# Taking 48 instead of 32 of 256 tokens out of the dense expert products, with GpSimd and ScalarE on the new 16, and first-key one-hots stored and reloaded

## The chip, the core and the metric

One Trainium2 chip, one core. The metric is the device time of the one launch in microseconds; lower is better.

## The reference

The network has three stages on 256 tokens of width 2048: an HGRN2 layer with a forgetting-attention layer, a second mixing layer (a gated linear recurrence and attention on selected keys), and a layer of product-key experts (PEER). The change is in the last one. Per token, 8 heads each choose 16 of 128 x 128 = 16384 experts by two keys of 128; each chosen expert is one row of `u` and one of `v`:

```python
expert = jnp.take_along_axis(cand_i, pos, axis=-1).reshape(t, -1)      # 128 of 16384 per token
gate = jax.nn.softmax(top_s, axis=-1).reshape(t, -1)
z = jnp.einsum('cd,ced->ce', xc, u[ec])
act = jax.nn.gelu(z, approximate=False) * gc
return jnp.einsum('ce,ced->cd', act, v[ec])
```

## The kernel before

**Dense tokens.** The kernel doesn't gather rows for most tokens. For the first DENSE = 224 tokens it computes z with *all* 16384 experts on TensorE, multiplies by a gate that is zero except at the chosen experts, and multiplies the result with all of `v`. The experts lie in four blocks of 32 units (BJ = 32; a unit is 128 experts x 2048 values, 1 MB fp32). The order is U0, U1, V0, U2, V1, U3, V2, V3; a U block makes z, the V block of the same number adds the output.

**A unit's way.** SP loads it into one of four buffers `raw` (`load`, L488), as soon as TensorE has finished the unit four before. ScalarE copies it to a rounded high half `wh` (L1344), VectorE subtracts to get the low half `wl` (L1856), and TensorE multiplies in single-pass fp32r: `dots` (L1142) has, per 128 rows, one matmul with `wh` and the high and low halves of x side by side (2 x 224 = 448 columns, L1153) and one with `wl` (224 columns, L1154). V0, V1 and V3 do the same (`wide_products`, L1201: L1206, L1207); V2 (`paired_v_block`, L1283) uses three matmuls of 224 columns (`value_products`, L1196 to L1198), two sums to a bank. Everything here has its own in-order queue per engine and meets by semaphores.

**Gates.** The gate of all experts of a block for 8 tokens is an outer product: `spread` (L1110) multiplies `hot_a` (one-hot of the first key, 128 slots x 8 tokens x 128 keys, fp16) with `gates_b` (one-hot of the second key within the block, times the gate) on TensorE, 8 matmuls of 64 columns, one turn ahead of each unit's products. With TURNS = 28 turns the 224 dense tokens of a block are done in 28 of 32 units. Gates of block b are spread during U(b+1), those of block 3 during V2. VectorE builds `hot_a`, `hot_b` and `gates_b` two turns ahead (`hot_rows`, L2534, `gate_rows`, L2547) and multiplies the spread gates onto the activations (`gate`, L2554), with ScalarE's copy of their low part (`keep_low_gates`, L1761). `hot_a` doesn't depend on the block, and is made anew in each.

**The last 32 tokens** (LAST) go by rows. Four groups of 32 partitions hold them, each group 32 of a token's 128 experts (ROWS = 32). `fetch_row` (L624) has GpSimd gather half rows (128 x 4 KB, into one of two buffers), and VectorE's `take_row` (L2607) takes a dot product with x (for u) or adds the weighted row to a sum (for v): 128 such steps, at turns listed by hand in ROW_TURNS (L60). `row_sums` (L1134) adds the four groups by a matmul with `token_of`, `add_rows` (L2641) puts them into x; the lower half of the width during V2, the upper at V3's end.

In V blocks ScalarE's loop (`v_highs`, L1815) also copies the activations' high half a unit ahead (`act_high`), and VectorE's `v_turns` (L2690) has their low half. In U blocks GpSimd adds the two halves of z (`add_dots`, L618), ScalarE applies GELU (`gelus`, L1774).

## Time and profile before

| | us |
|---|---|
| median of 3 runs | 3151.75 |
| runs | 3145.31, 3151.75, 6184.49 |
| profiled execution: time | 3146.41 |
| profiled execution: span | 3144.4 |

The span runs from the first to the last instruction. Times in rows are from its start. In the trace, PE is TensorE's matmul stream, PEld its weight loads, DVE is VectorE, ACT is ScalarE, POOL is GpSimd, SPq and POOLq are queues that issue DMAs. A timeline row is one instruction (or several of one kind, merged, xN): start, length, engine, line, operation, output <- inputs, shapes, and in brackets the engine's idle time before it with what ended it. Lengths of matmuls include their overlap with the next, so the distance of two starts is the time that one costs.

The table by stretch has one row per stretch: from:to, its length, then busy time and number of instructions of PE, PEld, DVE, ACT and POOL, the granted TensorE clock as a share of full speed, the mean busy share of the 16 DMA engines, and GB/s. A group row ends with busy us, mean ns of one, and idle time before.

### The profile page before, as it was taken

How to read it: one execution, taken by the hardware profiler on the slowest of the kernel's cores; microseconds unless marked ns; L12 is line 12 of the kernel's file. 1: busy time of each engine (PE TensorE's matmuls, PEld its weight loads, DVE VectorE, ACT ScalarE, POOL GpSimd, SP SyncE). 2: the span in 40 equal slices, each digit the busy share in tenths (PEclk: the TensorE clock that was granted, in tenths of full speed). 3: DMA queues.
4: the chain of work that ended last, by engine and by line, in shares of the span. 5: the costliest groups of instructions: out<-in, count | busy, mean ns of one | idle time of the engine just before them, and what ended most of it. 6: DMA issues, size and time to landing. Idle time of an engine off the chain costs nothing.

```text
span 3144.4 us, 62060 instructions
## 1 busy us (share of the span) xinstructions
PE 3106.8 (99%) x24748; PEld 3003.6 (96%) x24748; DVE 2407.6 (77%) x3908; ACT 1743.9 (55%) x2400; POOL 308.2 (10%) x303
## 2 busy tenths in 40 slices
PE   9999999999999999999999999999999999999998
PEld 9999999999999999999999988999999999999997
DVE  8767777755556776666668999988799789988887
ACT  6444545777776655555655455554555545554454
POOL 2000000000000000000000022331133112210110
PEclk9999999999999999999999999999999999999999
DMA  5444435444444545555455555678867787665785
GB/s 203 147 160 148 169 115 211 161 169 163 160 164 171 185 168 182 176 180 177 164 188 180 185 199 202 245 264 287 297 236 251 274 287 249 244 214 188 259 291 194
DMA packets 117821, 637.37 MB, mean 203 GB/s; under 512 B 11633, under 2 KB 32497, under 8 KB 50417
## 3 DMA queue, kind: packets, MB, share of 16 engines
q1 hardware_dynamic: 98496, 565.49, 50.7%
q0 software_dynamic: 18864, 68.43, 6.7%
q8 instruction: 121, 1.98, 0.2%
q10 hardware_dynamic: 288, 1.05, 0.1%
q14 instruction: 52, 0.42, 0.0%
HBM read 632.57 MB, written 2.36 MB: 202 GB/s over the span
## 4 chain that ended last, share of the span: by engine, by line
PE 86%; DVE 8%; DVEq 2%; ACT 2%; DMA 1%; issue 1%; ACTq 0%; SPq 0%
PE bank L670 14%; PE bank L672 14%; PE bank L671 14%; PE bank L1153 11%; PE bank L1206 9%; PE bank L1154 5%; PE bank L1207 5%; DVE wl L1856 3%; PE bank L1196 2%; PE bank L1198 2%; PE bank L1197 2%; PE bank L1117 1%; PE bank L824 1%; PE bank L1156 1%; ACT wh L1344 1%
## 5 line engine op out<-in xcount | busy, mean ns | idle before, releaser
L1856 DVE TENSOR_TENSOR wl<-raw,wh 128x1024 fp32r<-128x1024 f32 x1052 | 1267.1, 1238 | 349.9 <-ACT wh L1344 341.1
L1344 ACT ACTIVATE wh<-raw 128x1024 fp32r<-128x1024 f32 x1052 | 1052.7, 1050 | 394.3 <-DMA raw<-w_in_a 128.6
L671 PE MATMUL bank<-hhl,wh 128*128 128x256 f32 x3568 | 989.1, 277 | 0.0
L670 PE MATMUL bank<-hhl,wh 128*128 128x256 f32 x3440 | 966.9, 281 | 1.0 <-DVE hhl L1904 1.0
L672 PE MATMUL bank<-hhl,wl 128*128 128x256 f32 x3440 | 953.4, 277 | 0.0
L671 PEld LDWEIGHTS bank<-hhl,wh 128*128 128x128 f32 x3568 | 673.4, 189 | 1.9 <-issue 1.7
L670 PEld LDWEIGHTS bank<-hhl,wh 128*128 128x128 f32 x3440 | 647.9, 188 | 5.1 <-issue 2.4
L672 PEld LDWEIGHTS bank<-hhl,wl 128*128 128x128 f32 x3440 | 647.2, 188 | 0.0
L1153 PE MATMUL bank<-hhl,wh 128*128 128x448 f32 x1920 | 625.0, 382 | 6.8 <-DVE wl L1856 6.7
L1154 PE MATMUL bank<-hhl,wl 128*128 128x224 f32 x2048 | 522.4, 265 | 0.0
L1206 PE MATMUL bank<-ahl,wh 128*128 128x448 f32 x1488 | 472.1, 374 | 2.4 <-DVE ahl L2570 2.1
L1153 PEld LDWEIGHTS bank<-hhl,wh 128*128 128x128 f32 x1920 | 361.5, 188 | 40.6 <-DVE wl L1856 7.3
L1207 PE MATMUL bank<-ahl,wl 128*128 128x224 f32 x1536 | 400.1, 266 | 0.0
L1154 PEld LDWEIGHTS bank<-hhl,wl 128*128 128x128 f32 x2048 | 392.0, 191 | 2.8
L1206 PEld LDWEIGHTS bank<-ahl,wh 128*128 128x128 f32 x1488 | 279.5, 188 | 26.6 <-DVE ahl L2570 4.1
L1207 PEld LDWEIGHTS bank<-ahl,wl 128*128 128x128 f32 x1536 | 293.1, 191 | 1.5
L622 POOL TENSOR_TENSOR act<-z_parts 128x224 f32<-128x224 f32 x64 | 61.9, 967 | 1966.2 <-ACT z_parts L1785 1966.1
L1785 ACT ACTIVATE z_parts<-bank 128x448 f32<-128x448 f32 x128 | 69.8, 545 | 274.5 <-PE bank L1156 272.2
L670 PE MATMUL bank<-kh,wh 128*128 128x256 f32 x528 | 150.7, 285 | 0.0
L672 PE MATMUL bank<-kh,wl 128*128 128x256 f32 x528 | 147.0, 278 | 0.0
L671 PE MATMUL bank<-kl,wh 128*128 128x256 f32 x528 | 147.0, 278 | 0.0
L1196 PE MATMUL bank<-ahl,wh 128*128 128x224 f32 x512 | 142.8, 279 | 0.0
(461 smaller groups left out, 4405.2 us busy)
## 6 DMA issues: line engine op xcount, KB each, us to landing
raw<-peer_u SPq DMA_DIRECT2D x128, 1024.0 KB
raw<-peer_v SPq DMA_DIRECT2D x128, 1024.0 KB
raw<-w_in_c SPq DMA_DIRECT2D x64, 1024.0 KB
raw<-w_in_a SPq DMA_DIRECT2D x63, 1024.0 KB
raw<-w_kv SPq DMA_DIRECT2D x32, 1024.0 KB
raw<-w_in_b SPq DMA_DIRECT2D x32, 1024.0 KB
raw<-w_out_a SPq DMA_DIRECT2D x16, 1024.0 KB
raw<-w_out_b SPq DMA_DIRECT2D x16, 1024.0 KB
```

Source lines behind the costliest of these rows:

```text
L670: eng.matmul(out, h_[:, k, :], high[:, k, :], start=(k == 0), stop=False)
L671: eng.matmul(out, h_[:, k, :], low[:, k, :], start=False, stop=False)
L672: last = eng.matmul(out, low_rows(c, k), high[:, k, :], start=False, stop=(k == KC - 1))
L1153: eng.matmul(wide, wh[c % RAW][:, k, :], hhl[:, :, k, 0:DENSE], start=(k == 0), stop=False)
L1154: last = eng.matmul(wide[:, 0:DENSE], low_rows(c, k), hd[:, k, :], start=False, stop=False)
L1196: eng.matmul(out_, w_h, a_h, start=opens and e == 0, stop=False)
L1197: eng.matmul(out_, w_h, a_l, start=False, stop=False)
L1206: eng.matmul(wide, w_h, both, start=first, stop=False)
L1207: last = eng.matmul(wide[:, 0:DENSE], w_l, a_h, start=False, stop=False)
L1344: eng.activation(high_half(c, half), raw_half(c, half), ACT.Copy).then_inc(hi_ready, 1)
L1785: eng.activation(z_parts[:, c % 2, :], B[DOT_BANK[b] + c % 2][:, 0:2 * DENSE], ACT.Copy).then_inc(s["z_step"], 1)
L1856: eng.tensor_tensor(low_half_out(c, half), raw_half(c, half), high_half(c, half).bitcast(F32), ALU.subtract).then_inc(lo_ready, 1)
```

## The change

- MORE = 16 further tokens leave the dense products: DENSE is 208, TURNS 26. Matmuls of 448 columns have 416, those of 224 have 208.
- The 16 tokens go by rows, in 8 groups of 16 partitions (16 experts each, MORE_ROWS = 16), 64 gathers of 128 half rows into a single buffer `rows_more`. For u, GpSimd multiplies the 1024 columns with `x_more` (`more_dot`) and ScalarE sums the product with a copy's accumulator; for v, ScalarE scales the row and GpSimd adds it (`more_sum`). The steps stand at turns of the V blocks given by MORE_TURNS: 20 in V0, 21 in V1, 13 in V2, 10 in V3. ScalarE's part (`weigh_more`) comes at the end of its turn and waits for GpSimd's.
- SP copies keys and gates of these tokens in 16 small DMAs ahead of U1, and their x in 8 ahead of V0. Small tables move into the unused columns of `ahl`.
- `hot_a` is built in block 0's turns only. SP stores each tile (256 KB) to DRAM during U1, and reloads it in U2, U3 and V2 (`store_hot`, `load_hot`). A reload for turn n - 2 is issued behind the load of unit n; `spread` waits for it.
- The row sums of the new tokens are 8 more matmuls in each `row_sums`.
- Some semaphores of an earlier stage are merged into counting ones.

```diff
-DENSE = T - LAST
+MORE = 16
+MORE_GROUPS = P // MORE
+ROWED = LAST + MORE
+DENSE = T - ROWED
 TURNS = DENSE // TG
 ROWS = SLOTS_PER_TOKEN // GROUPS
+MORE_ROWS = SLOTS_PER_TOKEN // MORE_GROUPS
+ALL_ROWS = ROWS + MORE_ROWS
 ROW_TURNS = {
...
+MORE_TURNS = {
+    "V0": [n for n in range(BJ) if n % 8 in (0, 2, 3, 5, 6)],
+    "V1": [n for n in range(16) if n % 4 != 3] + [n for n in range(20, 30) if n != 24],
+    "V2": [n for n in range(13) if n % 2 == 0] + [n for n in range(20, BJ) if n % 2 == 0],
+    "V3": [n for n in range(23) if n % 5 in (0, 2)],
+}
...
+            def store_hot(n):
+
+                eng.wait_ge(sQ["pairs_ready"], n + 1)
+                eng.sem_inc(sp_passed, 1)
+                eng.dma_start(hot_rows_of[n], hot_tile(n)).then_inc(hot_stored[n % 2], 16)
+
+            def load_hot(b, n):
+
+                if (b, n) == (1, 0):
+                    for k in range(2):
+                        eng.wait_ge(hot_stored[k], 16 * (TURNS // 2))
+                eng.wait_ge(sQ["g_done"], b * TURNS + n - 1)
+                eng.sem_inc(sp_passed, 1)
+                eng.dma_start(hot_tile(n), hot_rows_of[n]).then_inc(hot_in[n % 2], 16)
+
+            def block_with_hot(name, table, b):
+
+                last = BLOCKS - 1 if name == "V" else b - 1
+                for n in range(BJ):
+                    load(n // PER_PAIR, BASE[f"{name}{b}"] + n % PER_PAIR, one(table, b * BJ + n))
+                    if 2 <= n < TURNS + 2 and last == 0:
+                        store_hot(n - 2)
+                    elif 4 <= n < TURNS + 2:
+                        load_hot(last, n - 2)
+                    elif TURNS + 2 <= n < TURNS + 4 and last < BLOCKS - 1:
+                        load_hot(last + 1, n - 2 - TURNS)
+
...
+                if (name, b) == ("U", 1):
+                    eng.wait_ge(sQ["x_out"], 16)
+                    eng.wait_ge(sQ["slots_step"], 1)
+                    eng.sem_inc(sp_passed, 1)
+                    for q in range(MORE_GROUPS):
+                        slots = slice(q * MORE_ROWS, (q + 1) * MORE_ROWS)
+                        eng.dma_start(row_keys[q * MORE:(q + 1) * MORE, :, ROWS:ALL_ROWS],
+                                      place[P - ROWED:P - LAST, NT - 1, :, slots]).then_inc(sQ["keys_in"], 16)
+                        eng.dma_start(row_gate[q * MORE:(q + 1) * MORE, ROWS:ALL_ROWS],
+                                      tops[P - ROWED:P - LAST, NT - 1].rearrange("p h k -> p (h k)")[:, slots]).then_inc(sQ["keys_in"], 16)
...
+            def fetch_more(g):
+
+                kind, r = g // MORE_ROWS, g % MORE_ROWS
+                eng.indirect_dma_start(out=rows_more[:, :], out_offset=None, in_=peer_u_rows if kind < 2 else v_rows,
+                                       in_offset=bass.IndirectOffsetOnAxis(ap=left[kind // 2][:, kind % 2, ROWS + r:ROWS + r + 1], axis=0)).then_inc(more_in, 16)
+
+            def more_dot(g):
+
+                kind, r = g // MORE_ROWS, g % MORE_ROWS
+                eng.wait_ge(more_in, 16 * (g + 1))
+                if g > 0:
+                    eng.wait_ge(sQ["more_by_scalar"], g)
+                if r == 0 and kind == 0:
+                    eng.wait_ge(sQ["more_x_in"], 16 * MORE_GROUPS)
+                if r == 0 and kind == 1:
+                    eng.wait_ge(sQ["x_out"], 16 + 16 * MORE_GROUPS)
+                eng.tensor_tensor(more_scaled[:, :], rows_more[:, :], x_more[:, :], ALU.mult)
+                eng.drain().then_inc(sQ["more_by_gpsimd"], 1)
...
+                fetch_more(g + 1)
...
+            def more_sum(g):
+
+                r = g % MORE_ROWS
+                in_place, ends = g in MORE_IN_PLACE, r == MORE_ROWS - 1
+                eng.wait_ge(sQ["more_by_scalar"], g + 1)
+                if not in_place and not ends:
+                    fetch_more(g + 1)
+                if r > 0:
+                    eng.tensor_tensor((rows_more if ends else x_more)[:, :], (rows_more if in_place else more_scaled)[:, :], x_more[:, :], ALU.add)
+                eng.drain().then_inc(sQ["more_step" if ends else "more_by_gpsimd"], 1)
+                if in_place and not ends:
+                    fetch_more(g + 1)
...
+                if b > 0:
+                    eng.wait_ge(hot_in[c % 2], i * (16 * PER_PAIR // 2) + 16 * (((b - 1) * TURNS + c) // 2 + 1))
...
+                eng.wait_ge(s["more_step"], f + 4)
+                for c in range(FH):
+                    eng.matmul(B[bank][:, FH * LAST + c * MORE:FH * LAST + (c + 1) * MORE], rows_more[:, c * P:(c + 1) * P],
+                               token_more[:, :], start=True, stop=True)
...
+            def weigh_more(b, n):
+
+                if (f"V{b}", n) in MORE_AT:
+                    g = MORE_AT[f"V{b}", n]
+                    kind, r = g // MORE_ROWS, g % MORE_ROWS
+                    if kind < 2:
+                        eng.wait_ge(s["more_by_gpsimd"], g + 1)
+                        eng.activation(more_scaled[:, :], more_scaled[:, :], ACT.Copy,
+                                       accum_out=row_dot[:, kind, ROWS + r:ROWS + r + 1]).then_inc(s["more_by_scalar"], 1)
+                    else:
+                        eng.wait_ge(more_in, 16 * (g + 1))
+                        if kind == 2 and r == 0:
+                            eng.wait_ge(s["more_step"], 3)
+                        elif r > 1 and g not in MORE_IN_PLACE:
+                            eng.wait_ge(s["more_by_gpsimd"], g - (kind - 2))
+                        out_ = x_more if r == 0 else rows_more if g in MORE_IN_PLACE else more_scaled
+                        eng.activation(out_[:, :], rows_more[:, :], ACT.Copy, scale=row_act[:, ROWS + r:ROWS + r + 1]).then_inc(s["more_by_scalar"], 1)
...
-                eng.tensor_tensor(hot_a[c % 2][:, :, :, :], iota_h[:, :, :].unsqueeze(1).broadcast_to(ka),
-                                  token_pairs[:, 0].unsqueeze(2).broadcast_to(ka), ALU.is_equal)
+                if b == 0:
+                    if n > 1:
+                        eng.wait_ge(hot_stored[c % 2], 16 * (n // 2))
+                    eng.tensor_tensor(hot_a[c % 2][:, :, :, :], iota_h[:, :, :].unsqueeze(1).broadcast_to(ka),
+                                      token_pairs[:, 0].unsqueeze(2).broadcast_to(ka), ALU.is_equal)
```

## Rows read from the trace of the kernel before

**Rows 1.** The page, busy time by engine, and the chain that ended last.

```profile
PE 3106.8 (99%) x24748; PEld 3003.6 (96%) x24748; DVE 2407.6 (77%) x3908; ACT 1743.9 (55%) x2400; POOL 308.2 (10%) x303
...
PE 86%; DVE 8%; DVEq 2%; ACT 2%; DMA 1%; issue 1%; ACTq 0%; SPq 0%
```

**Rows 2.** Stretches: busy us (instructions) by engine, granted clock, DMA share; U0 to V3.

```profile
1764.40:1940.90 176.50, 169.69 (x1065) 157.14 (x1063) 163.49 (x394) 93.50 (x141) 32.13 (x36) 0.99 0.56 195
1940.90:2113.00 172.10, 172.06 (x1250) 159.97 (x1249) 159.31 (x251) 97.03 (x158) 62.25 (x50) 1.00 0.70 248
2113.00:2275.00 162.00, 161.70 (x1024) 153.25 (x1024) 130.21 (x172) 81.62 (x97) 29.80 (x30) 1.00 0.84 292
2275.00:2447.00 172.00, 172.00 (x1249) 159.97 (x1248) 162.99 (x248) 95.85 (x155) 58.97 (x49) 1.00 0.71 250
2447.00:2609.30 162.30, 162.17 (x1025) 153.26 (x1024) 128.74 (x150) 81.57 (x98) 23.65 (x23) 1.00 0.79 279
2609.30:2781.30 172.00, 172.00 (x1252) 160.06 (x1252) 161.31 (x228) 96.23 (x155) 50.45 (x46) 1.00 0.69 246
2781.30:2963.60 182.30, 182.30 (x1777) 181.72 (x1777) 158.58 (x244) 87.69 (x126) 8.49 (x8) 1.00 0.58 204
2963.70:3129.00 165.30, 163.30 (x1042) 154.93 (x1040) 134.65 (x155) 86.70 (x111) 24.76 (x23) 1.00 0.74 259
```

**Rows 3.** Timeline of PE in V0: start us, length, ...; 448 and 224 columns in turn.

```profile
2149.90 0.37 PE L1206 MATMUL bank<-ahl,wh 128*128 128x448 f32 x1
...
2152.40 0.37 PE L1206 MATMUL bank<-ahl,wh 128*128 128x448 f32 x1
```

**Rows 4.** Timeline of PE in V2, 24 matmuls of 224 columns.

```profile
2899.75 0.27 PE L1196 MATMUL bank<-ahl,wh 128*128 128x224 f32 x1
...
2902.32 0.27 PE L1198 MATMUL bank<-ahl,wl 128*128 128x224 f32 x1
```

**Rows 5.** Timeline of PE: two of 512 columns and what follows; 13 of 256.

```profile
632.37 0.39 PE L879 MATMUL bank<-sum_h,ones_r 128*128 128x512 f32 x1
...
632.84 0.20 PE L657 MATMUL bank<-ones 128*128 128x64 f16 x1
...
1000.05 0.28 PE L670 MATMUL bank<-hhl,wh 128*128 128x256 f32 x1
...
1001.47 0.28 PE L670 MATMUL bank<-hhl,wh 128*128 128x256 f32 x1
```

**Rows 6.** Timelines of SP, ACT and PE: weight loads, issued and used.

```profile
1097.15 0.33 SPq L494 DMA_DIRECT2D raw<-w_iquery  x1
...
1101.94 2.01 ACT L1344 ACTIVATE wh<-raw 128x1024 fp32r<-128x1024 f32 x2 [2.44 <-DMA raw<-w_iquery]
...
2334.56 0.24 PE L1117 MATMUL bank<-gates_b,hot_a 128*128 128x64 f16 x2
...
2334.96 0.33 SPq L494 DMA_DIRECT2D raw<-peer_u  x1
...
2341.41 1.06 ACT L1344 ACTIVATE wh<-raw 128x1024 fp32r<-128x1024 f32 x1 [0.69 <-DMA raw<-peer_u]
```

**Rows 7.** Timelines of POOL and DVE: GpSimd's adds, and subtractions with and without them.

```profile
12.71 1.29 POOL L603 TENSOR_TENSOR sq<-first_sq 128x512 f32<-128x512 f32 x1 [3.67 <-ACT first_sq L1353]
...
19.27 5.75 POOL L603 TENSOR_TENSOR sq<-sq,first_sq 128x512 f32<-128x512 f32 x3 [5.28 <-ACT first_sq L1353]
...
23.79 3.44 DVE L1856 TENSOR_TENSOR wl<-raw,wh 128x1024 fp32r<-128x1024 f32 x2
...
2206.91 2.36 DVE L1856 TENSOR_TENSOR wl<-raw,wh 128x1024 fp32r<-128x1024 f32 x2
```

**Rows 8.** Timelines of POOL and DVE: one gather, issued and used.

```profile
2439.77 1.69 POOL L631 DMA_INDIRECT rows<-peer_u_rows,row_of  x1 [1.54 <-DVE rows L2618]
...
2443.36 1.23 DVE L2618 SCALAR_TENSOR_TENSOR rows<-rows,x_half 128x1024 f32<-128x1024 f32 x1 [1.58 <-DMA rows<-peer_u_rows,row_of]
```

**Rows 9.** Groups of DVE instructions in U2: the first-key compares.

```profile
L2544 DVE TENSOR_TENSOR hot_a<-iota_h,slotT 128x1024 f16<-128x1024 f16 x28 | 19.0, 680 | 0.0
```

More of the change, by code:

```diff
@@ L72 @@
         ROW_AT[_k, _n] = len(ROW_AT)
+assert len(ROW_AT) == 4 * ROWS
+MORE_TURNS = {
[4 more added lines that the diff above has]
+}
+MORE_AT = {}
+for _k, _v in MORE_TURNS.items():
+    for _n in _v:
+        MORE_AT[_k, _n] = len(MORE_AT)
+assert len(MORE_AT) == 4 * MORE_ROWS
+MORE_GELU_AT = 17
+MORE_GATED_AT = 17
+MORE_IN_PLACE = range(MORE_AT["V2", 0], MORE_AT["V3", 0])
 X_ROWS_AT = 9
```

189 lines of the change are left out of this document (126 added, 63 removed).

## The prediction

> **What bounds the kernel now.** I read the page first: TensorE is busy for 99% of the span and holds 86% of the chain that ended last, VectorE 8% of it [rows 1]. A TensorE that is always busy need not bound every stage, so the next view is the table by block of the expert stage [rows 2], cut where TensorE changes from one block of tables to the next (in order U0, U1, V0, U2, V1, U3, V2, V3). The reader is to see three kinds of stage. In U0 TensorE is busy 169.7 of 176.5 us and VectorE 163.5: VectorE's routing is the chain there. In U1, U2 and U3 TensorE is full and VectorE is nearly full too (159.3 to 163.0 of 172). In V0, V1, V2 and V3 TensorE is full, VectorE has 20% spare and the DMA queues are busiest (0.84 in V0). The granted clock is 1.00 in all (the 2.4 GHz level; 0.99 in U0). The 1,764 us before U0 aren't touched but for renamed semaphores, which I cost at nothing: each step waits for the same producer.
>
> **TensorE's columns.** In U0 to U3, V0, V1 and V3 the work is pairs of one 448-column and one 224-column matmul. From the first row of [rows 3] to the last lie eight pairs in 2.50 us: 313 ns a pair. They become 416 and 208 columns. What a wide column costs: two matmuls of 512 columns take 0.47 us together [rows 5], 235 ns each; of the 313 ns, if the narrow one has about 104, the wide one has 209. So 64 columns cost 26 ns, and 32 fewer save 13 ns. What a narrow column costs: 12 matmuls of 256 columns take 1.42 us [rows 5], 118 ns each; 23 of 224 take 2.57 us [rows 4], 112 ns each. So 32 columns cost 6.6 ns and 16 save 3 ns; the bounds are 0 and 6.5 ns (the wide rate). A pair saves 13 + 3 = 16 ns (13 to 20). A unit has 16 pairs: 0.26 us (0.21 to 0.32). The paired block V2 has only 224-column matmuls, 48 a unit: 0.15 us.
>
> The Trainium skill ("TensorE: Matmul & The Clock Gate", LDWEIGHTS) has a weight load of 128 columns take about columns / 1.2 GHz, 107 ns, whatever the moving operand's width. By it the narrow matmuls, at 112 ns in [rows 4], would save nothing, and the sum below would be some 12 us later. The trace agrees in part only: narrowing from 256 to 224 columns gained 6.6 ns, less than the wide rate of 13.
>
> **U0 and U1.** U0 follows VectorE's routing, which isn't changed: only the routing reaches over 27 of its 32 units, and only the last five can follow TensorE: 5 x 0.26 = **-1.3 us** (0 to -8.2, if all did). A U block is 28 turns with a spread of gates and 4 without; 172.0 = 28 x 5.42 + 4 x 5.06, with 5.06 from V0 (162.0 / 32) [rows 2]. Afterwards there are 26 turns of 5.16 and 6 of 4.80: 163.0 us, -9.0. In U1 the first-key compares are still made, and each tile is stored: VectorE loses only two of 28 turns of gating, so it stays near 155 us busy, and waits for a store now stand in its queue (the store goes out behind a weight load one turn earlier). I take **-7** (-9 to 0). The 16 small copies that SP issues before U1's first load fall where SP waits for the fourth unit before last; even 16 x 0.33 us, the length of an issue in [rows 6], stays inside the three units of lead, so nothing.
>
> **U2, U3 and V2: reloading.** The first-key tile of a turn (256 KB) is now loaded from SP, right behind the weight load of two units later. Both wait for the end of a unit, and TensorE needs the tile one unit after that. A weight load of 1 MB took 4.8 us from issue to ScalarE's start where nothing competed (1097.15 to 1101.94) [rows 6]. In U2 TensorE starts a spread at 2334.56, SP issues the load at 2334.96, and ScalarE, which waited for it, starts at 2341.41 [rows 6]: 6.4 us with a row gather under way. 256 KB more at the quiet load's own rate is at most 1.2 us, at 400 GB/s 0.6; I take 0.6. So the tile is there 0.4 + 4.8 + 0.6 = 5.8 us after the unit's end on a quiet turn, and 7.5 us with a gather. TensorE wants it after 5.16. This wait is new, it stands on TensorE's own queue, and everything behind it is dots of the unit.
>
> The wait isn't paid in full each turn, because a late spread gives the next tile more time: on quiet turns the length settles at (5.16 + 5.8) / 2 = 5.49 us, and a gather on every second turn makes two turns 5.16 + 7.5 = 12.64. U2 and U3 gather on every second turn. All quiet: 26 x 5.49 + 6 x 4.80 = 171.5 us. All colliding: 13 x 12.64 + 28.8 = 193.1. The middle is 182.3, so **+10.3 us each**. V2 is 182.3 now, 5.74 a turn; its matmuls give 5.59, and 5.23 without a spread. Quiet turns become 5.70; ten turns fetch rows, and a pair with one is 13.07 us if it collides, 11.41 if not. Quiet: 179.7; colliding: 196.3; middle 188.0, **+5.7**. The compares that leave VectorE in these blocks buy nothing by themselves, but they are cover: with VectorE at 163.0 in U2 [rows 2] TensorE could not have gone below that.
>
> The rule that would undo this is order in the queue. The Trainium skill ("DMA: Bandwidth & Descriptors", Queues, rings and completion order) has descriptors of one ring consumed in ring order, so a small load behind a large one waits for it; by that the 0.6 us stands on top. No row here shows 256 KB right behind 1 MB.
>
> **V0, V1 and V3: GpSimd's multiplies.** 64 more gathers bring 64 more halves of rows, worked by GpSimd (32 multiplies, 30 adds of 1024 columns) and ScalarE (a copy of 1024 columns each, 1.06 us by the last row of [rows 6]; it is busy 81.6 of 162 in V0 [rows 2], so 20 x 1.06 fits). What GpSimd does to VectorE is the price. At the start GpSimd adds 512 columns in 1.29 us alone [rows 7]; with VectorE working, three take 5.75 us, and VectorE's two subtractions beside them take 3.44 us where two take 2.36 [rows 7]. So a 512-column add costs VectorE 1.08 us, and one of 1024 twice that, 2.1 (0 if it falls in idle time, 2.6 if GpSimd's whole time is lost). V0 has 20, V1 20, V2 12, V3 10.
> The Trainium skill ("SBUF — State Buffer", two separate sides) calls the port that the two share an exclusive lock held for a whole instruction. By that each multiply would cost its full length, 2.6 us, and V0 10 us more; the row shows 1.08 of 1.29, most of it.
>
> V0: VectorE 130.2 - 1.3 (narrower) + 20 x 2.1 = 171 us; TensorE 162.0 - 8.2 = 153.8. VectorE becomes the bound. Some multiplies will fall in its 32 us of idle time, so I take 169: **+7** (-8 to +9). V1: 128.7 - 1.3 + 42 = 169; I take 168, **+6**. V3: 134.7 - 1.3 + 21 = 154 against TensorE's 165.3 - 8.2 = 157.1: **-8.2**. V2 has 158.6, loses 26 compares of 0.68 us [rows 9] and gains 25: 166 of 182, hidden.
>
> **The end.** The second row sum now has 8 more fp32 matmuls of 16 columns, 16 instructions; at the 112 ns of the narrowest stream that I have [rows 4] that is 1.8 us, and one more small add on VectorE makes **+2.1** (1 to 4). The first lies in V2, within its middle.
>
> **Sum**, against the profiled execution (span 3144.4, time 3146.4): -1.3 - 7 + 7 + 10.3 + 6 + 10.3 + 5.7 - 8.2 + 2.1 = +24.9, so **3171 us**, 0.6% above the median of the runs (3151.75). A difference under 2%, 63 us, is about what a measurement here can't tell from none.
>
> **Rivals.**
> 1. *Tiles in time and multiplies hidden.* TensorE sets every block: -1.3 - 3 x 9.0 - 3 x 8.2 - 5.6 + 2.1 = -56, **3090 us**; with the wide rate for narrow columns 3075. For it: TensorE's 99%, and GpSimd's idle time. Against it: 5.8 us against 5.16 on the quietest turn.
> 2. *Every gather collides, and GpSimd's chain of rows falls behind* (slower, on the other side). Its single buffer makes a cycle of fetch and multiply: a fetch issued at 2439.77 was used at 2443.36 [rows 8], 3.6 us, and a multiply of 2.6 us with about 1 us of waiting makes 7.2. V1's first 16 turns want 12 rows, one in 6.4 us. It decides when the cycle passes 6.4: then ScalarE waits, and weights with it, 12 x 0.8 = 10 us. With U2 and U3 at 193.1, V2 at 196.3 and V0 and V1 at 171: +25 + 2 x 10.8 + 8.3 + 2 + 10 + some of the same in V0 = about +70, **3215 us**.
> 3. *The narrow matmuls give nothing, all else as forecast*: 3183 us, inside the forecast's range.
>
> **How the numbers follow.** The forecast's mixture (with rival 3) gets 0.5, with its own range 3145 to 3200. Rival 1, wholly or halfway, 0.28; rival 2 0.22. Faster by over 2% means below 3089: less than half of rival 1, 0.12. Slower means above 3215: half of rival 2, 0.12. The rest, 0.76, is within 2%. The range that leaves out 2 in 10 is 3088 to 3222.
>
> **What would show it.** Wide matmuls in pairs of 297 ns. In U2 and U3, TensorE idle ahead of the spread's first weight load, released by a DMA into hot_a, 0.3 to 2.3 us, on nearly every turn; a turn of 5.5 us or more. If that wait is missing, the reload's price is wrong and rival 1 gains 26 us. In V0, VectorE over 160 us busy, its 1024-column subtractions and dot products with means well over 1.2 us, and TensorE waiting for the low halves; if VectorE stays under 150, the contention is mis-sized. ScalarE idle for GpSimd's product in V1's first half would show rival 2. U0 should stay within 2 us of 176.5.

## The result, and the profile after

The changed kernel takes 3341.6 us (median of 4 runs, 3331.9 to 3359.7), the one before 3150.9 beside it: a ratio of 1.062, 95% interval 1.056 to 1.068. The forecast was 3171 us with a range up to 3222, and its rival on the slower side stood at 3215: the kernel is slower than either by over 100 us. The profiled execution has a span of 3333.2 us. From its page, the busy times and the chain that ended last, to be laid beside [rows 1]:

```profile
PE 3121.4 (94%) x24716; PEld 3049.5 (91%) x24716; DVE 2398.5 (72%) x3794; ACT 1794.2 (54%) x2489; POOL 551.9 (17%) x439
...
PE 59%; DVE 13%; issue 10%; DMA 7%; POOLq 3%; DVEq 3%; POOL 3%; ACT 2%; SPq 1%; ACTq 0%
```

TensorE went from 99% busy to 94% and holds 59% of the chain in place of 86%. The blocks, in the columns of [rows 2], from U0 to V3:

```profile
1761.10:1937.50 176.40, 164.75 (x1065) 158.38 (x1063) 160.22 (x392) 89.82 (x137) 32.29 (x36) 0.98 0.56 193
1937.50:2107.80 170.30, 164.69 (x1233) 159.36 (x1232) 157.83 (x243) 99.29 (x160) 57.25 (x51) 1.00 0.87 302
2107.80:2327.20 219.40, 174.73 (x1033) 168.28 (x1033) 142.51 (x170) 96.52 (x134) 111.65 (x77) 0.89 0.74 261
2327.20:2509.20 182.00, 165.65 (x1229) 159.09 (x1225) 138.70 (x214) 94.50 (x156) 60.09 (x53) 1.00 0.80 283
2509.20:2732.70 223.50, 171.75 (x1032) 166.08 (x1032) 148.17 (x145) 102.31 (x133) 96.69 (x64) 0.91 0.72 253
2732.70:2920.50 187.80, 170.42 (x1232) 163.99 (x1232) 138.37 (x197) 92.02 (x152) 59.81 (x48) 0.97 0.75 258
2920.50:3129.10 208.60, 189.29 (x1775) 187.02 (x1771) 152.88 (x210) 102.33 (x140) 50.90 (x31) 0.97 0.68 241
3129.10:3319.10 190.00, 170.92 (x1056) 165.96 (x1056) 153.22 (x160) 94.88 (x121) 65.67 (x44) 0.94 0.71 250
```

V0 and V1 gained 57 and 61 us over [rows 2]; there no engine is near full, the DMA share is lower than before, and the granted clock has fallen to 0.89 and 0.91. Something waits. The waits of V0, longest first (us in total, times, longest):

```profile
ACT more_scaled L1974 <- POOLq L737: 107.2, 19, 9.7
POOL more_scaled L736 <- DMA rows_more<-peer_u_rows,left: 54.5, 17, 6.9
...
DVE ahl L2751 <- ACT ahl L1953: 48.5, 10, 8.7
PE bank L1358 <- DVE ahl L2751: 48.1, 17, 6.3
```

Read from below: TensorE waits for the low halves of the activations, VectorE for their high halves, ScalarE, which makes these, for line 737, and that is GpSimd's drain behind its multiply. So the row work of the 16 tokens sets the pace of the block. One turn of it, GpSimd and ScalarE in V0 (start, length, in brackets the idle time before and what ended it):

```profile
2143.40 2.39 POOL L736 TENSOR_TENSOR more_scaled<-rows_more,x_more 128x1024 f32<-128x1024 f32 x1 [3.84 <-DMA rows_more<-peer_u_rows,left]
2146.04 1.06 ACT L1974 ACTIVATE more_scaled<-more_scaled 128x1024 f32<-128x1024 f32 x1 [6.67 <-POOLq L737]
2146.77 0.97 POOL L723 DMA_INDIRECT rows_more<-peer_u_rows,left  x1 [0.98 <-issue]
...
2148.05 1.02 POOL L715 DMA_INDIRECT rows<-peer_u_rows,left  x1 [0.30 <-issue]
...
2154.57 2.58 POOL L736 TENSOR_TENSOR more_scaled<-rows_more,x_more 128x1024 f32<-128x1024 f32 x1 [5.50 <-DMA rows_more<-peer_u_rows,left]
```

From multiply to multiply 11.2 us: 2.4 of multiply, 1.0 until the gather's issue, 7.8 until it has landed. From the first of V0's twenty multiplies (2122.10) to the last (2328.7) 19 such turns take 10.9 us each. On average over them the multiply has 2.6 us, the stretch from its end to the next gather's issue 2.4 (0.9 to 6.5), and the landing 5.8 (4.2 to 8.1). The three leave 0.1 us of the turn for anything else: GpSimd's chain is closed, and 20 x 10.9 = 218 us is the length of V0.

And a long wait is paid again by the clock. The same block's end, ScalarE and TensorE:

```profile
2282.88 1.06 ACT L1974 ACTIVATE more_scaled<-more_scaled 128x1024 f32<-128x1024 f32 x1 [5.79 <-POOLq L737]
...
2284.20 0.71 PE L1358 MATMUL bank<-ahl,wh 128*128 128x416 f32 x1 [5.61 <-DVE ahl L2751]
...
2284.88 0.59 PE L1358 MATMUL bank<-ahl,wh 128*128 128x416 f32 x1
2285.44 0.59 PE L1358 MATMUL bank<-ahl,wh 128*128 128x416 f32 x1
...
2290.52 0.37 PE L1358 MATMUL bank<-ahl,wh 128*128 128x416 f32 x1
2290.82 0.37 PE L1358 MATMUL bank<-ahl,wh 128*128 128x416 f32 x1
```

After 5.6 us of idleness a pair of matmuls takes 0.56 us for some 5.7 us, then 0.30 again. A mean granted clock of 0.89 over V0 is 0.22 of 219 us, 48 us, at the 1.2 GHz level. These are seven stretches, and each begins in or just behind a wait of 3.5 to 6.3 us. TensorE is busy 174.7 us there for work that takes it 154.5 us in e4, below. So V0's 48 us of TensorE waits come with some 20 us of slow work.

### The profile page after: what moved, and what is told of

It is laid out like the page before. It is cut to its first block, busy times and chain, and to the rows that moved or that the text cites. A ratio compares the mean times of both kernels' runs of the same rounds, so it can differ in the third digit from the quotient of the medians.

```text
span 3333.2 us, 62035 instructions
## 1 busy us (share of the span) xinstructions
PE 3121.4 (94%) x24716; PEld 3049.5 (91%) x24716; DVE 2398.5 (72%) x3794; ACT 1794.2 (54%) x2489; POOL 551.9 (17%) x439
## 4 chain that ended last, share of the span: by engine, by line
PE 59%; DVE 13%; issue 10%; DMA 7%; POOLq 3%; DVEq 3%; POOL 3%; ACT 2%; SPq 1%; ACTq 0%
PE bank L816 13%; PE bank L817 13%; PE bank L818 13%; DVE wl L2034 5%; PE bank L1305 5%; DMA hot_a<-hot_rows_of 3%; PE bank L1306 2%; POOLq L737 2%; DMA rows<-peer_v,left 2%; POOL rows L715 1%; DVE x_half L2807 1%; PE bank L1348 1%; PE bank L1350 1%; PE bank L1349 1%; PE bank L1358 1%
## 5 line engine op out<-in xcount | busy, mean ns | idle before, releaser
L2034 DVE TENSOR_TENSOR wl<-raw,wh 128x1024 fp32r<-128x1024 f32 x1052 | 1295.9, 1264 | 368.2 <-ACT wh L1496 360.3
L1305 PE MATMUL bank<-hhl,wh 128*128 128x416 f32 x1920 | 603.6, 376 | 12.0 <-DVE wl L2034 11.4
L1358 PE MATMUL bank<-ahl,wh 128*128 128x416 f32 x1488 | 495.4, 391 | 120.7 <-DVE ahl L2751 118.5
L1306 PE MATMUL bank<-hhl,wl 128*128 128x208 f32 x2048 | 513.2, 261 | 0.0
L1358 PEld LDWEIGHTS bank<-ahl,wh 128*128 128x128 f32 x1488 | 300.4, 202 | 137.5 <-DVE ahl L2751 132.7
L1359 PE MATMUL bank<-ahl,wl 128*128 128x208 f32 x1536 | 406.6, 270 | 0.0
L706 POOL TENSOR_TENSOR act<-z_parts 128x208 f32<-128x208 f32 x64 | 62.6, 979 | 1992.7 <-ACT z_parts L1937 1992.7
L1359 PEld LDWEIGHTS bank<-ahl,wl 128*128 128x128 f32 x1536 | 314.3, 205 | 0.2
L1937 ACT ACTIVATE z_parts<-bank 128x416 f32<-128x416 f32 x128 | 66.2, 517 | 272.4 <-PE bank L1308 272.3
L1348 PE MATMUL bank<-ahl,wh 128*128 128x208 f32 x512 | 143.8, 281 | 0.0
```

The lines of the kernel that those rows point to most:

```text
L1305: eng.matmul(wide, wh[c % RAW][:, k, :], hhl[:, :, k, 0:DENSE], start=(k == 0), stop=False)
L1306: last = eng.matmul(wide[:, 0:DENSE], low_rows(c, k), hd[:, k, :], start=False, stop=False)
L1348: eng.matmul(out_, w_h, a_h, start=opens and e == 0, stop=False)
L1358: eng.matmul(wide, w_h, both, start=first, stop=False)
L1359: last = eng.matmul(wide[:, 0:DENSE], w_l, a_h, start=False, stop=False)
L1937: eng.activation(z_parts[:, c % 2, :], B[DOT_BANK[b] + c % 2][:, 0:2 * DENSE], ACT.Copy).then_inc(s["z_step"], 1)
```

## The experiments

Two theories stood at the start. A: the one-buffer chain of GpSimd (gather, multiply, drain, next gather) is too slow for its turns, and ScalarE's wait for it in order holds the block. B: the reload of hot_a and its traffic is the cost. All ratios are to the kernel before. e2, e4, e5, e8, e9, e10, e12 and e15 leave work out, as the text ahead of each result says, and are there only for their times.

| kernel | us | ratio, 95% | V0 | U2 | V1 | U3 | V2 | V3 |
|---|---|---|---|---|---|---|---|---|
| before | 3150.9 | 1 | 162.3 | 171.7 | 162.6 | 171.9 | 182.2 | 165.2 |
| changed | 3341.6 | 1.062 (1.056-1.068) | 219.3 | 182.1 | 223.5 | 187.8 | 208.6 | 189.9 |
| e1 no drain | 3308.5 | 1.050 (1.048-1.052) | 197.4 | 186.5 | 209.6 | 190.3 | 210.1 | 194.1 |
| e2 no rows of the 16 | 3163.3 | 1.004 (1.003-1.006) | 159.4 | 186.0 | 158.0 | 187.6 | 190.7 | 160.0 |
| e3 hot_a rebuilt | 3302.4 | 1.050 (1.047-1.052) | 210.6 | 176.4 | 224.9 | 174.6 | 190.6 | 196.8 |
| e4 columns only | 3126.7 | 0.993 (0.992-0.995) | 156.3 | 170.0 | 156.7 | 173.4 | 181.4 | 157.9 |
| e5 small operations | 3323.8 | 1.055 (1.051-1.058) | 204.2 | 187.8 | 213.2 | 184.1 | 207.9 | 195.5 |
| e6 two buffers | 3258.4 | 1.035 (1.033-1.037) | 187.7 | 188.7 | 182.9 | 184.4 | 205.5 | 179.4 |
| e7 = e6, hot_a rebuilt | 3206.5 | 1.019 (1.017-1.021) | 185.6 | 171.8 | 181.0 | 175.2 | 191.7 | 176.3 |
| e8 = e2, reload by GpSimd, late | 3217.9 | 1.022 (1.020-1.025) | 157.2 | 214.6 | 155.8 | 206.7 | 185.2 | 157.6 |
| e9 = e7, half gathers in V0 | 3204.5 | 1.019 (1.016-1.022) | 184.0 | 173.4 | 181.8 | 175.1 | 185.2 | 183.2 |
| e10 = e8, a turn earlier | 3125.5 | 0.992 (0.991-0.994) | 157.6 | 170.8 | 159.6 | 169.1 | 181.4 | 164.2 |
| e11 = e7, rows spread | 3222.5 | 1.023 (1.021-1.024) | 174.9 | 187.6 | 177.5 | 188.2 | 192.7 | 187.7 |
| e12 = e7, small operations | 3173.9 | 1.008 (1.005-1.011) | 178.6 | 171.5 | 171.1 | 174.9 | 183.2 | 171.8 |
| e13 = e6, reload as e10 | 3223.8 | 1.024 (1.021-1.026) | 184.7 | 168.9 | 178.9 | 171.3 | 211.4 | 180.0 |
| e14 = e7, one drain back | 3249.4 | 1.033 (1.031-1.034) | 212.5 | 170.8 | 193.7 | 176.0 | 190.3 | 180.3 |
| e15 = e12, half gathers in V0 | 3175.4 | 1.008 (1.005-1.011) | 175.0 | 169.4 | 169.7 | 175.2 | 183.2 | 174.8 |

The blocks are of the one profiled execution each, cut where TensorE changes block; that execution lies within 9 us of the kernel's median, in e8 14 us below it. So a block's difference of one or two us says little.

### The change taken apart: e2, e3, e4

e2 drops the row work of the 16 tokens:

```diff
-                        fetch_more(0)
...
-                        take_more(MORE_AT[f"{name}{b}", n])
...
-                    weigh_more(b, n)
```

> Left out: all row work of the 16 new tokens (gathers, GpSimd's multiplies and additions, ScalarE's sums and scalings, their transposition), so that their expert sums are missing; the narrower matmuls and the reload of hot_a stay. Theory 'GpSimd's chain of one buffer': V0 and V1, 219 and 223 us in the changed kernel, fall to 155 to 160, V3 to 158, V2 to 175 to 190, U2 and U3 keep what the reload costs them, 175 to 188; 3110 us, 3085 to 3135. Rival 'the reload and the traffic are the cost': V0 and V1 keep most of their length and the time stays over 3200 us.

e3 undoes the store and the reload, so that VectorE compares in every block again; e4 does both (the lines are shortened where three dots stand in them):

```diff
-                if b == 0:
-                    if n > 1:
-                        eng.wait_ge(hot_stored[c % 2], 16 * (n // 2))
-                    eng.tensor_tensor(hot_a[c % 2]...)
+                eng.tensor_tensor(hot_a[c % 2]...)
```

> The whole computation. Only the store and the reload of hot_a are undone: VectorE compares again in every block, 680 ns a turn. Theory 'the waits for hot_a and for the weights behind it lengthen U2, U3 and V2 (182, 188 and 203 us)': these lose 8 to 15 us each, 3310 us, 3295 to 3325. Rival 'their length is VectorE's and ScalarE's order': 3335 to 3350, and slower by VectorE's 19 us a block where it is the bound.

> Left out as in the run without the 16 tokens' row work, and hot_a is rebuilt by VectorE in every block: what is left of the change is 208 columns in place of 224. Theory 'a pair of matmuls takes 297 ns in place of 313': every unit 0.26 us shorter where TensorE is the bound, 3085 to 3100 us. Rival 'narrow matmuls give nothing' or other engines bound these blocks: 3130 to 3150 us.

The row work is worth 3341.6 - 3163.3 = 178 us, the reload 3163.3 - 3126.7 = 37 (39 with the rows, by e3), and the narrower matmuls give back 22 against the kernel before (3148.3 in those runs). Theory A names the main loss, B a real one of about a sixth. Both e2 and e4 came out above their expected ranges. For e2, this is the reload at SyncE in U2 (start, length):

```profile
2325.83 0.41 PE L1255 MATMUL bank<-gates_b,hot_a 128*128 128x64 f16 x8
...
2331.24 0.33 SPq L530 DMA_DIRECT2D raw<-peer_u  x1
...
2331.68 0.37 SPq L609 DMA_DIRECT2D hot_a<-hot_rows_of  x1
...
2338.08 0.40 PE L1255 MATMUL bank<-gates_b,hot_a 128*128 128x64 f16 x8 [1.21 <-issue]
```

By the order of loads and spreads, the tile issued at 2331.68 goes into the buffer that the spread of 2325.83 had freed, and is used at 2338.08, two spreads later. It could have been issued 5.8 us earlier; but ahead of it in SyncE's program stands the weight load of 2331.24, which waits for its own buffer. So the tile has 6.4 us to land, not 12, and TensorE waits: 39 us over the kernel. The profile puts half of that down to "issue", but there too the tile lands within 0.1 us before the spread starts (this one at 2337.99). In e4, where VectorE compares again, U2 has:

```profile
2262.00:2432.00 170.00, 164.75 (x1231) 158.99 (x1227) 162.85 (x241) 95.75 (x154) 59.73 (x50) 1.00 0.74 255
```

TensorE has less to do and isn't full any more; VectorE is busy 163 of 170 us. Seven of U2's later spreads wait 0.4 to 0.6 us for VectorE's `gates_b`. Narrower matmuls pay in V0, V1 and V3, 5.9 to 7.3 us each, but 1.7 us in U2, 0.8 in V2 and nothing in U3.

### The drain: e1, e5, e14

The changed kernel signals ScalarE by a drain, an instruction of its own behind the operation. e1 takes the signal from the operation itself, for the additions as for the multiplies:

```diff
-                eng.tensor_tensor(more_scaled[:, :], rows_more[:, :], x_more[:, :], ALU.mult)
-                eng.drain().then_inc(sQ["more_by_gpsimd"], 1)
+                eng.tensor_tensor(more_scaled[:, :], rows_more[:, :], x_more[:, :], ALU.mult).then_inc(sQ["more_by_gpsimd"], 1)
+                eng.wait_ge(sQ["more_by_gpsimd"], g + 1)
```

> The whole computation. Each GpSimd drain after a multiply or an addition of the 16 tokens' rows becomes a semaphore of that operation itself, for which GpSimd waits before it issues the next gather. In the trace of the changed kernel the drain in V0 ends with the multiply in 12 of 20 turns, and in the others 1.5 to 8 us later, within 0.2 us of the landing of the last gather that GpSimd issued (2183.30 to 2190.20, gather landed 2190.04; 2292.23 to 2300.59, landed 2300.10). Theory 'a drain waits for GpSimd's gathers in flight': some 1.2 us a row less in V0's 20 rows, 24 us, and a few us in V1, 3310 us in all. Rival 'what is late is the gather itself': the same instant is only a coincidence of a slow stretch, 3335 to 3342 us.

As expected, 33 us less; V0 lost 22. Its turn is 9.9 us: from the multiply's end to the next gather's issue 0.5 in place of 2.4, but the landings rose from 5.8 to 6.6. e5 keeps the drains and shortens the multiplies and additions to 64 columns:

> Left out: GpSimd's multiplies and additions for the 16 tokens work on 64 of their 1024 columns, and ScalarE sums x_more in place of the product, so that these tokens' sums are wrong; every gather, drain and wait stays, with the same numbers of instructions. In V0 of the changed kernel a row takes GpSimd some 10.9 us from multiply to multiply, of which the multiply is 2.4 and the gather's landing, with its issue, 6.0. Theory 'the cycle is a plain sum of landing, multiply, drain and issue': 2.1 us less for each of V0's 20 and V1's 11 dots, 42 and 23 us, and some 20 to 40 for the sums of V1 to V3: 3240 us, 3220 to 3270. Rival 'GpSimd's time is no part of it, the gathers alone pace the rows (full queue)': 3320 to 3340. Rival 'its operations slow VectorE, and that is the loss': VectorE's 1024-column operations in V0 fall to 1.20 us and V0 falls by 20 us or less.

Only 18 us came of the 100 expected. The time lies where the rival "the gathers alone pace the rows" had put it, and V0's 15 us would fit the other rival too; the trace says what paced them. GpSimd and ScalarE in e5's V0:

```profile
2157.47 0.93 POOL L715 DMA_INDIRECT rows<-peer_u_rows,left  x1 [0.30 <-issue]
2160.54 0.32 POOL L736 TENSOR_TENSOR more_scaled<-rows_more,x_more 128x64 f32<-128x64 f32 x1 [2.14 <-DMA rows_more<-peer_u_rows,left]
2167.29 1.06 ACT L1975 ACTIVATE more_scaled<-x_more 128x1024 f32<-128x1024 f32 x1 [8.59 <-POOLq L737]
2168.03 0.97 POOL L723 DMA_INDIRECT rows_more<-peer_u_rows,left  x1 [7.16 <-issue]
```

The operation ends at 2160.86, and ScalarE is told at 2167.3, 6.4 us later. In between GpSimd does nothing but drain. The gather issued at 2157.47, of the other 32 tokens, landed at 2167.14. In the trace of e5 17 of V0's 20 drains end 0.1 to 0.2 us after the later of the operation's end and the last landing among GpSimd's gathers. So with a short multiply the drain only waits longer, for a gather that has nothing to do with it. e14 puts one drain back into e7, where a gather is always in flight:

```diff
-                eng.tensor_tensor(more_bufs[k][:, :], ..., ALU.mult).then_inc(sQ["more_by_gpsimd"], 1)
+                eng.tensor_tensor(more_bufs[k][:, :], ..., ALU.mult)
+                eng.drain().then_inc(sQ["more_by_gpsimd"], 1)
```

> The whole computation. In the kernel with two buffers and hot_a rebuilt (3207 us) the multiply of each of the 32 dot rows is again followed by a drain that signals ScalarE, in place of the multiply's own semaphore; nothing else. There the gather of the next row has been issued just before each multiply. Theory 'a drain waits for the gathers that GpSimd has in flight': each product is told 4 to 5 us late, the landing (6.5 to 8 us) less the multiply's 2.4, and the second buffer is worth little: V0 from 186 to 195 to 215 us, V1 from 181 to 188 to 200, 3225 to 3260 in all. Rival 'a drain ends with the engine's own work': within 5 us of 3207.

3249.4 against 3206.5, 43 us, inside the range; V0 +27, V1 +13. Its V0, in the same columns:

```profile
2157.22 0.98 POOL L724 DMA_INDIRECT rows<-peer_u_rows,left  x1 [2.09 <-issue]
...
2158.51 1.01 POOL L735 DMA_INDIRECT rows_more<-peer_u_rows,left  x1 [0.30 <-issue]
2159.55 2.41 POOL L750 TENSOR_TENSOR more_scaled<-more_scaled,x_more 128x1024 f32<-128x1024 f32 x1
2167.01 1.06 ACT L1998 ACTIVATE more_scaled<-more_scaled 128x1024 f32<-128x1024 f32 x1 [4.55 <-POOLq L751]
```

The multiply ends at 2161.96, ScalarE hears of it at 2167.0, when the gather of 2158.51 has landed (2166.86).

### The landing: e6, e7

Multiplying and summing in place frees `more_scaled` as a second buffer, so the next row is fetched before this one is multiplied (in V2 one buffer stays). The drains are gone as in e1:

```diff
                 if g > 0:
                     eng.wait_ge(sQ["more_by_scalar"], g)
+                fetch_more(g + 1)
+                eng.wait_ge(more_in[k], count)
...
-                eng.tensor_tensor(more_scaled[:, :], rows_more[:, :], x_more[:, :], ALU.mult)
-                eng.drain().then_inc(sQ["more_by_gpsimd"], 1)
+                eng.tensor_tensor(more_bufs[k][:, :], more_bufs[k][:, :], x_more[:, :], ALU.mult).then_inc(sQ["more_by_gpsimd"], 1)
...
-                fetch_more(g + 1)
```

> The whole computation. GpSimd multiplies in place and ScalarE sums in place, so that more_scaled becomes a second buffer for the rows: the gather of a row is issued before the multiply of the row before it; in V2, where more_scaled is not free, one buffer stays. The drains are semaphores, as in the run without drains. Theory 'the row chain is latency: landing after multiply after landing': with the landing hidden a row costs GpSimd 2.4 plus some 2.5 us for two issues, less than the 8 us that V0 has for each of its 20, and V0 goes to 165 to 170, V1 to 165 to 175, V3 to 170 us: 3215 us in all, 3190 to 3240. Rival 'two gathers at a time slow each other and the weights so that the rate stays': V0 stays over 190, 3290 to 3310 us.

> The whole computation: two buffers as above, no drains, and hot_a rebuilt by VectorE in every block. If reload and row chain are separate losses, as the first four runs suggest (39 us with the rows, 37 without), this is 39 us below the run with two buffers: 3175 us, 3150 to 3200. Rival 'VectorE, which compares again, falls behind where it also shares its port with GpSimd': less than 20 us of the 39 come.

e6 is 50 us below e1: the landing is on the chain. But V0 stayed at 188, not 170, so both were above their ranges; e7 shows that the losses of the reload and of the rows don't only add, they cost 52 us here for 37 to 39 elsewhere.

### What is left in V0: e9, e12, e15

e9 halves 18 of V0's 20 gathers for the 16 tokens, in e7:

```diff
+                m = P // 2 if 2 <= g < MORE_AT["V1", 0] else P
-                eng.indirect_dma_start(out=more_bufs[k][:, :], ...
+                eng.indirect_dma_start(out=more_bufs[k][0:m, :], ...
```

> Left out: the kernel with two buffers and hot_a rebuilt, 3207 us, but 18 of V0's 20 gathers for the 16 tokens fetch the rows of 64 partitions in place of 128, so that the products of the others are made from old rows; the numbers of instructions and waits are the same. V0 there lasts 185.6 us with its 16 DMA engines busy 0.87 of the time, 161 us; in the kernel before it lasts 162 us at 0.84, 136 us. Theory 'with the chain hidden, V0 is paced by what its DMA engines must move': 4.7 MB less, some 11 us of engine time, and V0 falls by 8 to 14 us, 3195 in all. Rival 'the order of GpSimd and ScalarE still paces it': V0 within 4 us of 185.6.

The rival held: half the bytes of these gathers changed next to nothing (184.0 for 185.6). The groups of VectorE's instructions in V0 of e7 (busy us, mean ns):

```profile
L2055 DVE TENSOR_TENSOR wl<-raw,wh 128x1024 fp32r<-128x1024 f32 x64 | 90.3, 1450 | 6.6 <-ACT wh L1517 6.6
L2769 DVE TENSOR_TENSOR ahl<-act,ahl 128x416 fp32r<-128x416 f32 x31 | 35.6, 1147 | 10.2 <-ACT ahl L1974 10.2
```

and in e4, without the 16 tokens' rows:

```profile
L2007 DVE TENSOR_TENSOR wl<-raw,wh 128x1024 fp32r<-128x1024 f32 x64 | 75.9, 1226 | 28.7 <-ACT wh L1477 28.7
...
L2721 DVE TENSOR_TENSOR ahl<-act,ahl 128x416 fp32r<-128x416 f32 x31 | 18.1, 585 | 0.1
```

VectorE is busy 158.7 us against 126.6 for the same work: 32 us for 20 multiplies, 1.6 us each. e12 shortens GpSimd's operations in e7 to 64 columns:

> Left out: in the kernel with two buffers and hot_a rebuilt (3207 us), GpSimd's multiplies and additions for the 16 tokens work on 64 of 1024 columns, so that these tokens' sums are wrong; all gathers and waits stay. In V0 there VectorE is busy 158.7 us, against 134 to 142 where GpSimd's operations are absent or fall in its idle time: 64 subtractions of 1450 ns in place of 1226, and 31 of ahl at 1147 in place of 585. Theory 'GpSimd's operations cost by holding up VectorE, 1.6 us each': VectorE is back to some 134 us busy, ahl at 585, and V0 falls to 165 us or less, V1 and V3 by 8 to 15; 3165 us, 3150 to 3180. Rival 'the waits in order between GpSimd, VectorE and ScalarE are the cost': V0 stays over 178, 3190 or more.

33 us less, inside the range, and `ahl` is back at 599 ns. So with the chain hidden these operations do cost what they do to VectorE; V0 gave only 7 of it, V1 10, V2 8, and V0's 178.6 is the rival's value, not the theory's 165. V0 in e12, and ScalarE's wait there:

```profile
2103.90:2282.60 178.70, 162.03 (x1033) 159.60 (x1033) 130.26 (x172) 100.22 (x136) 73.03 (x79) 0.95 0.90 327
```

```profile
ACT wh L1517 <- DMA raw<-peer_v: 37.6, 21, 3.9
```

Now ScalarE waits for weights with the DMA engines busy 0.90, 161 us; before it was 0.84 of 162, 136 us. e15 combines e12 with e9's half gathers:

> Left out: as in the twelfth run (3174 us; GpSimd works on 64 of 1024 columns for the 16 tokens), and in V0 18 of the 20 gathers for them fetch 64 of 128 partitions. With short GpSimd operations V0 lasts 178.6 us at a DMA share of 0.90 and 327 GB/s, and ScalarE waits 37.6 us for weights. Theory 'what is left of V0's excess is the DMA engines' time': 4.7 MB less at 327 GB/s, V0 164 to 170 us. Rival 'it is the waits in order, the bytes are hidden': V0 175 to 180, as the ninth run found with long operations (184.0 against 185.6).

V0 is 175.0, at 306 GB/s with a share of 0.92: 5 MB less, and the engines no less busy. That is the edge of the rival's range and short of the theory's: the last 19 to 22 us of V0 over e4 stay open. The DMA engines are nearly full there, but their time doesn't follow the bytes.

### The reload from another queue: e8, e10, e13

GpSimd issues the reload in place of SyncE. The first condition below is e8's, the second e10's:

```diff
-                    elif 4 <= n < TURNS + 2:
-                        load_hot(last, n - 2)
...
+                if last > 0 and 1 <= n < TURNS - 1:
+                    load_hot(last, n + 1)
...
+                if last > 0 and n < TURNS - 2:
+                    load_hot(last, n + 2)
```

> Left out: the row work of the 16 tokens, as in the second run, 3163 us with SyncE's reload and 3127 with hot_a rebuilt. Here GpSimd issues the reload, as soon as the spread two turns before it is done, so that it doesn't queue behind a 1 MB weight load on SyncE and no weight load waits behind it. Theory 'the reload costs by its place in SyncE's one queue: it lands after its turn, and the weights behind it come late': U2, U3 and V2 fall from 186, 188 and 191 to 170 to 176, 172 to 178 and 180 to 186 us, 3125 to 3135 in all. Rival 'what costs is the traffic, 256 KB more a turn on the same 16 engines': 3155 to 3165.

> Left out: the row work of the 16 tokens, as in the second run (3163 us with SyncE's reload, 3127 with hot_a rebuilt). The eighth run's reload from GpSimd took its place one turn late: GpSimd issued a tile at 2341.84 that the spread of the very next turn wanted, 2346.82, and U2 rose to 214 us. Here each tile is issued a turn earlier, as soon as its buffer can be free. Theory 'the reload costs by its place in SyncE's one queue, 1 MB loads before and behind it': U2, U3 and V2 at 170 to 177, 172 to 178 and 180 to 187 us, 3125 to 3140 in all. Rival 'its traffic or the short time between its buffer's release and its use costs the same from any queue': 3155 or more.

e8 came out above both of its ranges. It placed each load where the very next turn wants it, and U2 rose to 215 us: a tile that comes a turn late costs more than one that shares a queue. e10, a turn earlier, makes the reload as cheap as the compares that it replaces (3125.5 against e4's 3126.7). A tile of e10, from the spread that frees its buffer to the spread that uses it:

```profile
2281.06 0.42 PE L1262 MATMUL bank<-gates_b,hot_a 128*128 128x64 f16 x8
...
2284.10 0.55 POOL L764 DMA_DIRECT2D hot_a<-hot_rows_of  x1
...
2293.81 0.41 PE L1262 MATMUL bank<-gates_b,hot_a 128*128 128x64 f16 x8
```

Issued 3.0 us after the first, it has 9.7 us to land. The 37 us were not the 20 MB but the late issue: the same bytes, from e8's queue but a turn earlier, cost nothing against e4.

> The whole computation: two buffers, no drains, and the reload of hot_a issued by GpSimd two turns ahead. Without the rows that reload cost nothing (3125 against 3127 us with hot_a rebuilt). If the losses add, this is within 10 us of the kernel with two buffers and hot_a rebuilt: U2, U3 at 169 to 173, V2 186 to 192, 3190 to 3210 us. Rival 'in V2, where GpSimd also gathers and adds for the 16 tokens, the reload is late again': V2 over 200 us, 3215 or more.

With the rows of the 16 tokens the rival held: U2 and U3 are at 169 and 171, but V2 at 211. GpSimd's queue is now where loads wait for TensorE's spreads, with the additions behind them, and TensorE in turn waits 15.8 us for tiles in V2. GpSimd's waits there; the first is 70.5 us in e7 too, the second is new:

```profile
POOL x_more L769 <- ACT rows_more L2016: 76.7, 11, 10.7
POOL hot_a L792 <- PE bank L1298: 46.1, 9, 12.0
```

### Rows in other blocks: e11

```diff
-    "V0": [n for n in range(BJ) if n % 8 in (0, 2, 3, 5, 6)],
+    "V0": [n for n in range(BJ) if n % 8 in (0, 3, 5)],
+    "U2": list(range(0, BJ, 4)),
...
+    "U3": list(range(0, BJ, 4)),
```

> The whole computation. Two buffers, hot_a rebuilt, and the 64 rows of the 16 tokens spread: V0 12 of its 20, U2 8, V1 15 of 21, U3 8, V2 11 of 13, V3 10. In the U blocks GpSimd multiplies and adds between its own additions and gathers again only two turns later or after ScalarE, so that nobody waits for a landing. Theory 'each V block takes as many rows as its DMA time and its chain hold, the rest is free in U, where the DMA engines are busy 0.71 and GpSimd 60 of 172 us': V0 168, V1 168, U2 and U3 some 3 to 5 us longer than 172 and 175 by VectorE's slower operations, 3165 in all, 3145 to 3180, so not below the kernel before by 2 percent in any case. Rival 'VectorE, busy 164 of 172 us in U2, is held back by each GpSimd operation and by ScalarE's sums': U2 and U3 over 182 us, 3190 or more.

The rival held, against e7. V0 went from 186 to 175 and V1 from 181 to 178, but U2 and U3 rose by 16 and 13. One view of e11, the groups of VectorE in U2:

```profile
L2767 DVE TENSOR_TENSOR hot_a<-iota_h,slotT 128x1024 f16<-128x1024 f16 x26 | 37.2, 1430 | 0.0
...
L2765 DVE TENSOR_TENSOR hot_b<-iota_h,slotT 128x256 f16<-128x256 f16 x26 | 15.8, 606 | 0.0
```

The compares of hot_a took 680 ns in [rows 9]; VectorE is busy 181 of 188 us. Eight multiplies added 17 us to the 164 of e7. No version found here with the 16 tokens' rows beats the kernel before.

## Why the prediction was wrong

**The step that failed: the turn of GpSimd's row chain, 7.2 us.** The forecast itself gave this chain no term: V0's 169 and V1's 168 are worked out from VectorE and TensorE alone. Only rival 2 priced it, with a turn of 3.6 + 2.6 + 1. Measured in V0, the turn is 10.9 us: 5.8 for the gather where 3.6 stood, 2.6 for the multiply as said, and 2.4 where "about 1 us of waiting" stood.

The 3.6 us came from a gather "issued at 2439.77" and "used at 2443.36" [rows 8]. Those two rows aren't a pair. The rows of the 32 tokens have two buffers, and `fetch_row(n)` is issued when row n - 2 has been taken; the row used at 2443.36 was fetched two uses earlier. In the trace of the kernel before, VectorE's and GpSimd's timelines:

```profile
2433.46 1.70 DVE L2618 SCALAR_TENSOR_TENSOR rows<-rows,x_half 128x1024 f32<-128x1024 f32 x1
...
2438.27 1.22 DVE L2618 SCALAR_TENSOR_TENSOR rows<-rows,x_half 128x1024 f32<-128x1024 f32 x1 [0.83 <-DMA rows<-peer_u_rows,row_of]
```

```profile
2431.54 1.69 POOL L631 DMA_INDIRECT rows<-peer_u_rows,row_of  x1 [3.17 <-DVE rows L2618]
...
2435.44 1.69 POOL L631 DMA_INDIRECT rows<-peer_u_rows,row_of  x1 [1.36 <-DVE rows L2618]
```

2431.54 to 2438.27 is 6.7 us, 2435.44 to 2443.36 is 7.9. With their mean, 7.3, the prediction's own sum gives 7.3 + 2.6 + 1.0 = 10.9 us a row and 218 us for V0. That this is the measured number is luck: V0's landings are shorter, and the drain's wait for gathers in flight, which no row of before shows, fills the place. Still, 7.3 would have shown that 20 rows don't fit; the mistake was to take the nearest issue above a use as its own. Rival 2 had the mechanism, and its test (ScalarE idle for GpSimd's product) is the largest wait of V0, 107.2 us, and 53.5 us in V1's first half, where rival 2 looked for it. But it was costed at 0.8 us a row, where the turn is 10.9 us against the 8.1 that V0 has for each of its 20 rows at 162 us.

This shows the chain, not all of V0: of the 63 us by which V0 exceeds e4's, taken off one after another, the drain's end brought 22 (e1), the second buffer 10 (e6), the rebuilt hot_a 2 (e7) and GpSimd's hold on VectorE 7 (e12). The last 22 are open.

**One link on.** Nothing in the prediction had a stall of TensorE cost more than its length. With the clock at 0.89, V0's waits of 48 us brought about 20 us more.

**By block.** Predicted and measured: U0 175.2 and 176.4; U1 165.1 and 170.3 (166.1 to 168.0 in the eight kernels without stores, 167.8 to 172.9 in the eight with them, so the stores cost a few us); V0 169 and 219.4; U2 182.3 and 182.0; V1 168 and 223.5; U3 182.3 and 187.8; V2 188.0 and 208.6 (190.7 without the rows, e2); V3 157.1 and 190.0. V2 and V3 were weighed by VectorE's and TensorE's budgets alone, again without the chain; what exactly V3's ten rows wait for is not taken apart here. Summed, and with 3.3 us gained before U0 and 3.4 at the end, the misses are the 164 us by which 3333.2 exceeds the 3169.3 predicted for the span; V0, V1, V2 and V3 hold 159 of them.

**Columns: right for the pairs, wrong for V2.** The pair went from 313 ns to 303, U1's timeline over ten pairs:

```profile
1938.60 0.37 PE L1305 MATMUL bank<-hhl,wh 128*128 128x416 f32 x1
...
1941.63 0.37 PE L1305 MATMUL bank<-hhl,wh 128*128 128x416 f32 x1
```

Medians over whole blocks are 317 and 302 in U1, 314 and 300 in V0 (e4), 14 to 15 ns where 16 were forecast. But the 3 ns of a narrow matmul by itself aren't there. V2 has nothing else, and in e4, where TensorE is full in it, 23 of 208 columns take what 23 of 224 took in [rows 4], 2.57 us:

```profile
2880.28 0.27 PE L1329 MATMUL bank<-ahl,wh 128*128 128x208 f32 x1
...
2882.85 0.27 PE L1331 MATMUL bank<-ahl,wl 128*128 128x208 f32 x1
```

V2 fell by 0.8 us where rival 1 had 5.6: there rival 3 was right. The whole kernel kept only 22 us of rival 1's 56, because VectorE stands right behind TensorE in U2 and U3, as e4 showed. With VectorE relieved as well (e10, 143 us busy) 23 of 25 turns of U2 take 5.15 to 5.17 us, the forecast's 5.16. Its 170.8 us in place of 163 are three single waits: 2.3 us for `gates_b` (spread of 2288.66), 3.0 for a tile (spread of 2333.1), and some 2 before V1's first matmul.

**The reload: right in kind and near in size.** U2 and U3 were forecast 10.3 us longer each; without rows they are 14.3 and 15.7 longer (e2). That U2 of the changed kernel hit its forecast to 0.3 us is partly luck: it is 182 to 189 us in the kernels with SyncE's reload. Still, the wait stands where it was said, ahead of the spread's weight load. The landing, 5.8 us after the unit's end and 7.5 with a gather, was near (e2's U2: 5.0 to 7.9 from issue to landing, 5.6 on average). What the prediction took as given, and what e2 and e10 showed to be the cause, is the issue at the unit's end: the buffer was free a turn earlier. By the Trainium skill ("DMA: Bandwidth & Descriptors", Queues, rings and completion order) descriptors of one ring are consumed in ring order, from which the prediction took that the small load waits for the large one. Here that was not the loss: tiles landed in 5.6 us on average behind weight loads, in e2's U2, and in 5.7 from GpSimd's queue, in e8's U2.

**The multiply's price for VectorE: right, and hidden.** 2.1 us each were forecast. In the changed kernel V0's VectorE is busy 142.5 us, 14 more than in e2 for 20 multiplies, probably because most fall while it waits; once the chain is hidden they cost 1.6 (e7) and, in a full U2, 2.1 (e11). The Trainium skill ("SBUF — State Buffer", two separate sides) has the shared port locked for the whole instruction, here 2.4 us; the measured 1.6 to 2.1 are most of that. One reading beside it was off: V2 was put among the blocks where VectorE has 20% spare and the DMA queues are busiest, but [rows 2] has 13% and a share of 0.58, the lowest but one. Nothing in the sum rests on it.
